# Modulation jobs of a two-layer diffusion trunk: one a chunk in p1, the rest in p2 and the first FFN quarter

## The reference

```python
for l in range(DEPTH):
    mod = (jax.nn.silu(cond) @ w_mod[l] + b_mod[l])[:, None, :]
    sh1, sc1, g1, sh2, sc2, g2 = jnp.split(mod, N_MOD, axis=-1)
    u = _ln_plain(x) * (1.0 + sc1) + sh1
    mix, st = _token_mixer(u, h0_all[:, l], grid, w_in[l], ...)
    x = _ln(DN_ALPHA * x + g1 * mix, ln1_g[l], ln1_b[l])
    u2 = _ln_plain(x) * (1.0 + sc2) + sh2
    if l % 2 == 0:
        f = _swiglu(u2, ffn_w1[l // 2], ffn_w3[l // 2], ffn_w2[l // 2])
    else:
        f = _moe(u2, router_w[l // 2], router_b[l // 2], moe_w1[l // 2], moe_w3[l // 2], moe_w2[l // 2])
    x = _ln(DN_ALPHA * x + g2 * f, ln2_g[l], ln2_b[l])
```

## Time and profile before

| | |
|---|---|
| runs, us | 4442.12, 4412.87, 4927.4 |
| median | 4442.12 |
| profiled execution | 4442.12, span of its slowest core 4440.5 |
| spans of the 8 cores | 4389.5 to 4440.5 |
| PE busy | 3569.5 us, 80% of the span |
| DVE, ACT, POOL busy | 40%, 21%, 8% |
| mean granted PE clock, slowest core | 0.881 of full |
| chain that ended last | PE 71%, DVE 13%, DMA 6%, issue 5%, ACT 5% |

### The profile page before, as it was taken

The page is one execution under the profiler, slowest core; times in us unless marked ns, Lnnn a source line. Parts: engine busy times, 40 slices in busy tenths (PEclk is TensorE's granted clock), DMA queues, the critical chain, the costliest instruction groups (busy, mean ns, idle before and its releaser), DMA issues.

```text
span 4440.5 us, 52000 instructions; the slowest of 8 cores (4389.5 to 4440.5 us)
## 1 busy us (share of the span) xinstructions
PE 3569.5 (80%) x18728; PEld 1820.5 (41%) x18728; DVE 1769.4 (40%) x2406; ACT 942.9 (21%) x1459; POOL 365.4 (8%) x427
## 2 busy tenths in 40 slices
PE   2453559389916666938999999999999999999992
PEld 1221225145413323524555554555554554555451
DVE  2444443632375665363232333232323323233327
ACT  2424331221125454121111110111111111111011
POOL 1111011000100001100000000000000000000000
PEclk9666679689957777968999999999999999999996
DMA  7455445044412323504444444444444444444331
GB/s 121 59 67 63 62 54 64 10 62 63 53 19 23 30 23 39 62 4 62 67 55 65 58 62 57 61 59 67 62 58 57 62 62 58 62 62 62 53 53 48
DMA packets 423161, 243.38 MB, mean 55 GB/s; under 512 B 164096, under 2 KB 391936, under 8 KB 422912
## 3 DMA queue, kind: packets, MB, share of 16 engines
q0 software_dynamic: 418160, 224.96, 40.1%
q1 hardware_dynamic: 4752, 15.10, 1.1%
HBM read 459.65 MB, written 5.32 MB: 105 GB/s over the span
## 4 chain that ended last, share of the span: by engine, by line
PE 71%; DVE 13%; DMA 6%; issue 5%; ACT 5%; DVEq 0%; SPq 0%; ACTq 0%; POOLq 0%
PE ps L114 71%; DVE s_reg L114 6%; DMA s_ring<-w_in 4%; DVE s_mv L114 3%; DVE s_xres L114 2%; ACT s_reg L114 2%; ACT s_tw L114 1%; DVE s_tw L114 1%; ACT L114 1%; DMA s_ring<-gwbd 1%; DVE s_ubuf L114 0%; DMA s_condt<-cond 0%; DMA s_ring<-w_mod 0%; DVEq L111 0%; ACT s_xres L114 0%
## 5 line engine op out<-in xcount | busy, mean ns | idle before, releaser
L114 PE MATMUL ps<-s_ubuf,s_ring 128*128 128x512 bf16 (+1 forms) x12192 | 2321.0, 354 | 234.8 <-DMA s_ring<-gwbd 164.2
L114 PEld LDWEIGHTS ps<-s_ubuf,s_ring 128*128 128x128 bf16 x12192 | 1219.7, 100 | 1327.8 <-issue 448.1
L114 DVE TENSOR_TENSOR s_reg<-ps,s_reg 128x512 bf16<-128x512 f32 (+3 forms) x786 | 469.4, 602 | 1693.9 <-PE ps L114 1689.1
L114 ACT ACTIVATE s_reg<-ps 128x512 f32<-128x512 f32 (+1 forms) x834 | 434.2, 527 | 2699.4 <-PE ps L114 2696.9
L114 PE MATMUL ps<-s_ring,s_reg 128*128 128x512 bf16 x4280 | 949.0, 384 | 51.7 <-DVE s_reg L114 51.7
L114 PEld LDWEIGHTS ps<-s_ring,s_reg 128*128 128x128 bf16 x4280 | 423.4, 99 | 561.1 <-issue 87.5
L114 DVE SCALAR_TENSOR_TENSOR s_reg<-ps,s_comb,s_reg 128x1024 f32<-128x1024 f32 x310 | 397.6, 1284 | 363.3 <-PE ps L114 363.2
L117 POOL DMA_DIRECT2D s_ring<-moe_w x208 | 179.7, 864 | 2257.6 <-PE ps L114 1776.6
L114 PE MATMUL ps<-s_reg,s_ring 128*128 128x512 bf16 (+1 forms) x960 | 229.7, 374 | 124.9 <-ACT s_reg L114 89.5
L114 PE MATMUL ps<-s_identb,s_tw 128*128 128x128 bf16 x320 | 40.5, 307 | 246.6 <-ACT s_tw L114 243.7
L114 DVE TENSOR_TENSOR s_reg<-s_reg 128x1280 f32<-128x1280 f32 (+2 forms) x112 | 124.5, 1112 | 246.1 <-ACT s_reg L114 236.6
(11 more groups left out here) (68 smaller groups left out, 990.4 us busy)
## 6 DMA issues: line engine op xcount, KB each, us to landing
s_ring<-moe_w POOLq DMA_DIRECT2D x176, 512.0 KB, 5.7
s_ring<-moe_w POOLq DMA_DIRECT2D x24, 1536.0 KB, 13.0
s_ring<-w_in POOLq DMA_DIRECT2D x112, 256.0 KB, 4.4
s_ring<-w_mod POOLq DMA_DIRECT2D x24, 1024.0 KB, 11.5
s_ring<-ffn_w POOLq DMA_DIRECT2D x22, 512.0 KB, 5.7
s_ring<-moe_w POOLq DMA_DIRECT2D x8, 1024.0 KB, 9.6
s_xres<-xin SPq DMA_DIRECT2D x1, 5120.0 KB, 22.9
yout<-s_xres SPq DMA_DIRECT2D x10, 512.0 KB, 2.6
```

The source lines that it names most:

```text
L114: getattr(eng, name)(*a, **kw).then_inc(sems[e], 1)
```

## The change

Jobs are placed by a function `mod_jobs_at(site)` instead of the table `mod_sched`: one job of layer 0 (4 to 11) after each chunk of p1; one job of layer 1 (0 to 7) after each piece of p2 in layer 0; jobs 8, 9, and 10 with 11, of layer 1 after the three f1 pieces of the first quarter of layer 0's FFN. Each job takes a PSUM bank of its own by `palloc(1)` and is finalized at once, with two DVE instructions (three for jobs 2, 3, 8 and 9). No bank is reserved in p1 any more. The weights loaded, the matmuls and their sizes are the same.

```diff
-        mod_sched = {}
-        for l in range(nl):
-            q = ([(0, n) for n in range(4, 12)] if l == 0 else []) + ([(l + 1, n) for n in range(12)] if l + 1 < nl else [])
-            for c in range(NCH):
-                mod_sched[(l, c)] = q[3 * c:3 * c + 3]
-            assert len(q) <= 3 * NCH
+        def mod_jobs_at(site):
+            kind, l = site[0], site[1]
+            if kind == 'p1' and l == 0:
+                return [(0, 4 + site[2])]
+            if kind == 'p2' and l + 1 < nl:
+                return [(l + 1, site[2])]
+            if kind == 'f1' and l + 1 < nl and site[2] == 0 and site[3] == 0 and site[4] in (0, 2, 4):
+                return [(l + 1, 8 + site[4] // 2)] + ([(l + 1, 11)] if site[4] == 4 else [])
+            return []
...
-        def mod_job(ml, n, bank, colbase):
+        def mod_job(ml, n):
+            bank = palloc(1)
             slot, skey = ring_next(('mod', ml, n))
             wv = slot[:, 0:8 * 512].rearrange("p (k n) -> p k n", k=8)
             for f4 in range(4):
-                f = n * 4 + f4
                 for k in range(8):
...
+            c_lo = n * 4
             for s_ in range(2):
-                dve(lambda e, s_=s_: e.tensor_tensor(out=mk(modT[:, 0:1], ml * 96 + c_lo * 2 + s_, [[2, n]]),
-                                                    in0=mk(ps[:, bank, 0:1], colbase + c_lo * 2 + s_, [[2, n]]),
-                                                    in1=spc(SP_BMOD + ml * 48 + c_lo, n), op=ALU.add), pk(bank) + ['smallp'], [('modT', ml)])
...
+                dve(lambda e, s_=s_: e.tensor_tensor(out=mk(modT[:, 0:1], ml * 96 + c_lo * 2 + s_, [[2, 4]]),
+                                                    in0=mk(ps[:, bank, 0:1], s_, [[2, 4]]),
+                                                    in1=spc(SP_BMOD + ml * 48 + c_lo, 4), op=ALU.add), pk(bank) + ['smallp'], [('modT', ml)])
+            if n in (2, 3, 8, 9):
+                dve(lambda e: e.tensor_scalar(out=modT[:, ml * 96 + c_lo * 2:ml * 96 + c_lo * 2 + 8], in0=modT[:, ml * 96 + c_lo * 2:ml * 96 + c_lo * 2 + 8],
+                                              scalar1=1.0, scalar2=None, op0=ALU.add), [('modT', ml)], [('modT', ml)])
...
-                pst['reserved'] = {MODB}
...
-                    for (ml, n) in mjobs:
-                        mod_job(ml, n, MODB, (ml % 2) * 96)
-                        if n == 11:
-                            mod_finalize(ml, 16 if ml == 0 else 0, 48, MODB, (ml % 2) * 96)
-
-                pst['reserved'] = set()
+                    for (ml, n) in mod_jobs_at(('p1', l, c)):
+                        mod_job(ml, n)
+
...
+                    for (ml, n) in mod_jobs_at(('p2', l, m)):
+                        mod_job(ml, n)
```

More of the change, by code:

```diff
@@ L343, in build_nc @@
                 pieces.append((('p1', l, c), mk_p1_piece(l, c)))
-                for (ml, n) in mod_sched[(l, c)]:
+                for (ml, n) in mod_jobs_at(('p1', l, c)):
                     pieces.append((('mod', ml, n), mk_mod_piece(ml, n)))
@@ L347, in build_nc @@
                 pieces.append((('p2', l, m), mk_p2_piece(l, m)))
+                for (ml, n) in mod_jobs_at(('p2', l, m)):
+                    pieces.append((('mod', ml, n), mk_mod_piece(ml, n)))
             for h in range(2):
@@ L353, in build_nc @@
                         pieces.append((('f1', l, e, q, i), mk_f1_piece(w1, w3, f0 + i, 2)))
+                        for (ml, n) in mod_jobs_at(('f1', l, e, q, i)):
+                            pieces.append((('mod', ml, n), mk_mod_piece(ml, n)))
                     pieces.append((('f2', l, e, q), mk_f2_piece(w2, f0, nf)))
@@ L492, in mod_job @@
             for f4 in range(4):
-                f = n * 4 + f4
                 for k in range(8):
-                    pe(lambda e, wv=wv, f4=f4, k=k, f=f: e.matmul(ps[:, bank, colbase + f * 2:colbase + f * 2 + 2], lhsT=wv[:, k, f4 * 128:(f4 + 1) * 128],
-                                                               rhs=scond[:, k * 2:k * 2 + 2], start=(k == 0), stop=(k == 7)),
+                    pe(lambda e, wv=wv, f4=f4, k=k: e.matmul(ps[:, bank, f4 * 2:f4 * 2 + 2], lhsT=wv[:, k, f4 * 128:(f4 + 1) * 128],
+                                                          rhs=scond[:, k * 2:k * 2 + 2], start=(k == 0), stop=(k == 7)),
@@ L497, in mod_job @@
                        [skey, 'scond'], pk(bank))
-        def mod_finalize(ml, c_lo, c_hi, bank, colbase):
-            n = c_hi - c_lo
+            c_lo = n * 4
             for s_ in range(2):
-                dve(lambda e, s_=s_: e.tensor_tensor(out=mk(modT[:, 0:1], ml * 96 + c_lo * 2 + s_, [[2, n]]),
-                                                    in0=mk(ps[:, bank, 0:1], colbase + c_lo * 2 + s_, [[2, n]]),
-                                                    in1=spc(SP_BMOD + ml * 48 + c_lo, n), op=ALU.add), pk(bank) + ['smallp'], [('modT', ml)])
[L505 to L508, removed]
@@ L510, in build_nc @@
-        MODB = 7
-        bm0 = palloc(1)
+                dve(lambda e, s_=s_: e.tensor_tensor(out=mk(modT[:, 0:1], ml * 96 + c_lo * 2 + s_, [[2, 4]]),
[4 more added lines that the diff above has]
+                                              scalar1=1.0, scalar2=None, op0=ALU.add), [('modT', ml)], [('modT', ml)])
@@ L512, in build_nc @@
         for n in range(4):
-            mod_job(0, n, bm0, 0)
-        mod_finalize(0, 0, 16, bm0, 0)
+            mod_job(0, n)
         try:
@@ L523, in build_nc @@
                 barrier(TWK, ('act', 'dve', 'pool'))
-                pst['reserved'] = {MODB}
                 for c in range(NCH):
                     slot, skey = ring_next(('p1', l, c))
-                    mjobs = mod_sched[(l, c)]
                     wv = slot[:, 0:5 * 1024].rearrange("p (g k n) -> p g k n", g=5, k=8)
@@ L766, in build_nc @@
                                         out=aq[:, fl, t0:t0 + tn], in0=ps[:, b3, 0:tn], in1=ts_[:, 0:tn], op=ALU.mult), pk(b3) + [tsk], [(aqk, i + fi, j)])
+                            for (ml, n) in mod_jobs_at(('f1', l, ei, q, i)):
+                                mod_job(ml, n)
                         slot, skey = ring_next(('f2', l, ei, q))
```

## The result

The changed kernel takes 0.9836 of the time of the kernel before, 95% interval 0.9767 to 0.9905; on another chip, in the run e9_changed below, 0.9838, 0.981 to 0.9867. The forecast was 4363 over 4442, 0.982. Its profiled execution took 4379.3 us, against the 4363 forecast and 4442.1 before. The median of all 12 runs is 4453.2 us (4338.0 to 5759.0), which lies above the stated range of 4333 to 4395; that of 12 runs of the kernel before is 4577.8. Seven of the changed kernel's twelve runs are slow ones, with a lower granted clock on one die or both, and the two ratios leave such runs of either kernel out. So the change is worth 1.6%, inside the 2% that the prediction gave as about what a measurement can tell from no change.

A forecast was written before the change was run, and what follows sets the result against it. In layer 0's p1, PE waits for loads held up by job slots; p2 is bound by PE. Terms -140.4 + 41 + 3 + 17 = -79.4 us took 4442.1 to 4363 us; range 4333 to 4395.

The forecast's parts named there:

- p1 in layer 0: Layer 0's p1: with one job a chunk, loads are hidden and it runs at layer 1's pace plus finalizing; -140.4 us.
- The 11 us of room for the load: Layer 0's p1: a piece's 38 us load is needed 49 us on, so it is hidden with 11 us to spare.
- the 2 us behind the bank: p1's third projection: PE's wait for a job's bank until DVE has finalized stays hidden, with 2 us left.
- p2 in layer 0: Layer 0's p2: a w_mod in each period and a late-freed slot lengthen the stage from 136.0 to 176.8 us; +41 us.
- The period: Layer 0's p2, time per piece: POOL's chain gives 22.9 us, the slot 22.2 or 23.7 with slow restart; 23.3 taken.
- w_o: After layer 0's p2: the second w_o piece waits for the slot of p2(7), so the first row block waits; +3 us.
- FFN: Layer 0's first FFN quarter: four jobs 4 us, f2's late load 10.6, PE's restart 2; f1 loads just fit; +17 us.
- the case I had called likeliest: Whole kernel: the forecast as summed, 4355 to 4380 us, chance 0.56.
- w_mod is cheap: Rival for p2: w_mod adds little to the next DMA, p2 +17 to +24, total 4339 to 4346 us; chance 0.26.
- w_mod is dear: Rival for p2: transfers share, period 25 to 28 us, f1 loads slip too, total 4380 to 4390 us; chance 0.08.
- p1 does not fall to layer 1's pace: Rival for layer 0's p1: late PE restart or loads over 49 us; 3 us a chunk gives 4387 us; chance 0.07.
- PE's clock: Rival for p2 and f1: pauses keep PE at its lower clock of 1.2 GHz, +166 us, total 4529 us; chance 0.03.

The follow-up runs named there:

- e9_changed: The changed kernel run again, unaltered, on another chip beside the kernel before; 0.9838 of that kernel's time, interval 0.981 to 0.9867.
- e2_batch: Changed kernel with layer 1's jobs moved to its own p1 and behind layer 0's last f2, jobs 4-11 finalized once per layer from a reserved bank; 0.9686 of kernel before.
- e8_half: Changed kernel with p2's eight w_mod pieces loaded by half, 512 KB each, so results differ from the reference; p2 173 to 179 us, mean 176.
- e6_warm: Changed kernel with 24 unused matmuls added behind the job of each of p2's pieces 0 to 6; p2 181 to 192 us, mean 186.
- e5_side: Changed kernel with p2's w_mod pieces in a buffer of their own, leaving all three ring slots to p2 pieces; p2 167 to 180 us, mean 173.

## Why the prediction was right or wrong

**p1 in layer 0**: right in cause and size: 405 to 406 us on every core where 405.9 was forecast, and -140.7 on core 5 against -140.4. The 11 us of room for the load held, and so did the 2 us behind the bank. The price of the finalizing was right: forecast 4.8 us a stage, measured 4.6 beyond layer 1's p1 without jobs, of which e2_batch took off 2.3 in layer 0, and 4.1 in layer 1.

**p2 in layer 0**: the mechanism was right (three slots, a round of two pieces, POOL's chain beside it), but this is the term of the sum that failed, by its size: +41 forecast, +54 measured in the mean and +60 on the core from which the rows were taken. Four parts of it failed, all the same way:

- *The price of w_mod.* I put 11.15 + 0.5 us from w_mod to the second DMA, the first number from six pairs of one core in p1. In p2 it is 12.2 over all cores and in both profiles of this kernel. The steps to the fourth DMA are 10.6 and not 10.3, and from its issue to PE's start 5.6 pass and not 5.3.
- *The period.* Of the two bounds I took a value between them, 23.3. They stood so close that both added: POOL lost 0.7 us a piece to the slot on top of its chain. The mean period was 23.6 to 25.1 us by core. Over six periods 8.9 us were missing on core 7.
- *The first piece.* p2(1) came 24.6 us into the stage on core 7, not 20.0: 8.9 us passed from its first to its second DMA where 7.1 were taken over from before, and its last took 7.4 us to PE's start with the next w_mod behind it, not 5.3. On three cores it did come at 19.5 to 20.6.
- *The last piece.* PE took 20.1 us for p2(7) and not 17.4. I had set the slow restart inside the period only, where the loads hide part of it; at the end nothing hides it.

4.6 + 8.9 + 2.7 make the 16 us between the end of p2(7) on core 7, 193.0 us into the stage, and its forecast, 176.8. In the mean of the cores they are 3.0 + 6.8 + 1.9.

**w_o**: forecast +3, measured -0.7 in the mean. The second w_o piece landed 10 us after the end of p2(7), as forecast, but at the moment it was needed; PE waited 0.17 us for it on core 7. The first row block started 6.8 us after p2's end, where 5.9 had been taken over from before, and its first 8 matmuls took 3.2 us and not 1.9.

**FFN**: right, +17 against +18 on core 5 and +20 in the mean; the wait of 11.4 us ahead of f2 (forecast 10.6) and 2 us of restart were as forecast; the f1 load that "just fits" missed by 1.4 us on core 7.

**The sum**: too low by 13 us from p2 in the mean; w_o gave 4 back, the FFN took 3 more and p1 1.5. The ratio of 0.984 beside the forecast 0.982 is inside the case I had called likeliest: -72 us by e9_changed (4334 against 4403 to 4409) where -79 was forecast. That 4379 came out so near to 4363 as a time is in part luck. The 4442.1 that I started from holds 35 us in layer 1's experts that the change has no part in: 2411 us on cores 4 and 5 at a granted clock of 0.967, 2376 on cores 0 to 3 at 0.981. The profile after has the like on cores 6 and 7, 2413 us at 0.965. Without it, in e9_changed, the changed kernel took 4334, at the lower edge of the range.

**The range** failed: the median of 12 runs, 4453.2, lay above it, and the 13 us of p2 are not what put it there. The step that failed is the last of the sum, "4442.1 us, which is also the median of the runs shown": I took the time of one execution for the level of all, and set the range by w_mod's price and 5 us for p1 and the FFN alone, though one of the three times shown was 4927.4. The twelve runs went from 4338 to 5759.

**The rivals**: *w_mod is cheap* was wrong, and e8_half shows why: its price goes with its bytes, 7.0 us for 1 MB. The section "Anatomy of one DMA — SWDGE (gpsimd) path" of the Trainium skill's page "DMA: Bandwidth & Descriptors" had led there, with an estimate of 2.4 us for 1 MB from its fit; the runs disagree for this load, which casts. Whether the cast is the reason no run here tests. *w_mod is dear* was half right: the lower end of its period, 25 us, occurred on two cores, and f1 slipped by 1.4 us. *p1 does not fall to layer 1's pace* did not occur. *PE's clock*: the granted clock fell from 0.97 to 0.86 in p2 (0.83 on core 5) and not to the lower level for good; e6_warm prices what reached the end at 2 to 5 us.

**Left open**: why p2 takes 182 us on one core and 199 on another in one execution, with the same program. The pairs from w_mod to w_in spread from 10.1 to 15.2 us. In e5_side cores 0, 2, 4 and 6 took 176.6 to 180.4 and their odd neighbours 167.1 to 170.8, and the order differs from run to run. The record shows a pattern in it. In both profiles of the changed kernel one core of each pair of neighbours (0 and 1, 2 and 3, 4 and 5, 6 and 7) takes 3 to 12 us longer in p2 than the other, now the even one and now the odd, and on the longer one w_b_out lands 5.4 to 6.3 us after its issue in the mean, on the shorter one 4.5 to 4.7. That speaks for something that two neighbours share, but no run here tests it.

## What to carry to other kernels

In a small ring of slots that is filled in program order, a piece's price is the change that it makes to who must be done before the next piece can load: one more piece for each chunk cost half a microsecond, two cost 12 to 18. Put side work where the bound is another engine and the period of the ring still lets the next piece in early; here that was each layer's own p1, and it gave 3.1% where the change as made gave 1.6%. Where two bounds come out within a microsecond of each other, add some of both, and price a DMA from all cores rather than from one. A range for a time needs the spread of the runs in it, and not only the doubts about the terms.

## What the runs showed of the hardware

A w_mod of 1 MB delayed the DMA behind it by some 7 us and half of it by 3.5: from its issue to the second DMA behind it 12.2 and 8.7 us passed, where the two DMAs alone are 5.0 to 5.5 apart. A row of waits grew by 81 us in name without costing anything: the same rest of PE was booked on ACT in one kernel and on DVE in the other. PE's first 16 matmuls after a wait of 1.4 to 14 us in p2 took 4.6 to 6.4 us in 53 of 56 pieces, at a granted clock of 0.64 in the one shown, and 3.6 where unused matmuls had filled the wait. The period of p2 differed by core, 23.6 to 25.1 us within one execution, which I had not expected of eight cores running one program.
